# Two transformer blocks in fp32 on one core: another order of work in the last projection, four products with the norm's weights on GpSimd, and weight sums in DRAM that pause

## The reference

```python
branch_d = jnp.einsum('nbsw,nwd->bsnd', ys, w_branch)
g = jax.nn.sigmoid(gates.reshape(bsz, s, N_BRANCH, d))
merged = jnp.sum(g * branch_d, axis=2)
h = x + merged @ w_out            # the last projection
out = rms_norm_2(h, final_g)      # h * rsqrt(mean(h*h) + eps) * final_g
```

## Time and profile before

| | |
|---|---|
| three runs | 1256.29, 1257.59, 1258.3 us; median 1257.59 |
| the profiled execution | 1253.7 us, of which the span of the trace is 1252.0 |
| granted clock, mean | 0.996 |
| busy | PE 1236.2 us, DVE 878.1, ACT 658.7, POOL 84.0 |

### The profile page before, as it was taken

One profiled execution on the slowest core, in us unless ns is written; L12 is line 12 of the kernel. 1 busy time (PEld: TensorE's weight loads), 2 busy tenths in 40 slices (PEclk: granted clock), 3 DMA queues, 4 the chain that ended last, 5 costly groups with the idle time before them and its releaser, 6 DMA issues.

```text
span 1252.0 us, 19450 instructions
## 1 busy us (share of the span) xinstructions
PE 1236.2 (99%) x7427; PEld 1086.2 (87%) x7427; DVE 878.1 (70%) x1560; ACT 658.7 (53%) x1235; POOL 84.0 (7%) x135
## 2 busy tenths in 40 slices
PE   9999999999999999999999999999999999999996
PEld 7887777899999998888888888888898899999985
DVE  5367776697766588788574788765786766665796
ACT  5366676455454455565644224663456774444643
POOL 1000000011010100001200101000000000000000
PEclk9999999999999999999999999999999999999998
DMA  7259888167667755655525888777898886554621
GB/s 253 102 170 252 233 228 223 65 236 232 149 202 226 221 164 179 211 208 185 192 80 162 241 261 239 201 202 235 270 297 270 256 257 223 194 202 169 248 88 68
DMA packets 42141, 253.27 MB, mean 202 GB/s; under 512 B 5304, under 2 KB 6588, under 8 KB 14144
## 3 DMA queue, kind: packets, MB, share of 16 engines
q1 hardware_dynamic: 27096, 161.12, 35.2%
q0 software_dynamic: 11808, 85.99, 28.2%
q10 hardware_dynamic: 3144, 4.92, 1.3%
HBM read 241.51 MB, written 81.80 MB: 258 GB/s over the span
## 4 chain that ended last, share of the span: by engine, by line
PE 92%; DVE 4%; issue 2%; ACT 1%; DMA 1%; POOL 0%; SPq 0%; POOLq 0%; DVEq 0%; ACTq 0%
PE bank L2395 22%; PE bank L2396 22%; PE bank L2397 22%; PE sc L2395 4%; PE sc L2396 4%; PE sc L2397 4%; PE sc L2571 3%; PE tp L2580 2%; PE ob L2637 1%; PE ob L2595 1%; DVE w_lo L1520 1%; PE bank L2512 1%; PE bank L2521 1%; DMA w_raw<-in_weights 1%; PE bank L2502 1%
## 5 line engine op out<-in xcount | busy, mean ns | idle before, releaser
L1520 DVE TENSOR_TENSOR w_lo<-w_raw,w_hi 128x512 fp32r<-128x512 f32 (+1 forms) x417 | 302.2, 772 | 131.6 <-ACT w_hi L910 130.7
L910 ACT ACTIVATE w_hi<-w_raw 128x512 fp32r<-128x512 f32 (+1 forms) x417 | 262.9, 688 | 140.9 <-PE bank L2397 92.3
L2395 PE MATMUL bank<-xT_hi,w_hi 128*128 128x256 f32 (+1 forms) x928 | 319.7, 345 | 0.3
L2397 PE MATMUL bank<-xT_hi,w_lo 128*128 128x256 f32 (+1 forms) x928 | 309.2, 333 | 0.0
L2396 PE MATMUL bank<-xT_lo,w_hi 128*128 128x256 f32 (+1 forms) x928 | 308.9, 333 | 0.0
L2395 PEld LDWEIGHTS bank<-xT_hi,w_hi 128*128 128x128 f32 x928 | 176.3, 190 | 20.3 <-issue 4.6
L2397 PEld LDWEIGHTS bank<-xT_hi,w_lo 128*128 128x128 f32 x928 | 176.1, 190 | 17.7
L2396 PEld LDWEIGHTS bank<-xT_lo,w_hi 128*128 128x128 f32 x928 | 176.5, 190 | 15.3 <-issue 1.0
L2395 PE MATMUL bank<-act_hi,w_hi 128*128 128x256 f32 (+1 forms) x400 | 124.4, 311 | 0.0
L2396 PE MATMUL bank<-act_lo,w_hi 128*128 128x256 f32 (+1 forms) x400 | 123.4, 308 | 0.0
L2397 PE MATMUL bank<-act_hi,w_lo 128*128 128x256 f32 (+1 forms) x400 | 123.3, 308 | 0.0
(11 more groups left out here) (365 smaller groups left out, 2364.5 us busy)
## 6 DMA issues: line engine op xcount, KB each, us to landing
w_raw<-in_weights SPq DMA_DIRECT2D x84, 1024.0 KB, 5.1
sum_dram<-in_weights POOLq DMA_DIRECT2D x54, 1024.0 KB, 8.7
w_raw<-sum_dram SPq DMA_DIRECT2D x34, 1024.0 KB, 4.8
sum_dram<-sum_dram POOLq DMA_DIRECT2D x18, 1024.0 KB, 6.8
arena<-in_weights SPq DMA_DIRECT2D x8, 1024.0 KB, 9.5
act_f<-in_weights POOLq DMA_DIRECT2D x6, 1024.0 KB, 9.9
arena<-in_weights POOLq DMA_DIRECT2D x4, 1024.0 KB, 11.5
act_lo<-act_lo SPq DMA_DIRECT2D x24, 128.0 KB, 5.6
```

What stands on the lines that cost most here:

```text
L910: nc.scalar.activation(w_hi[SPLIT_AT[b]][:, cols], w_raw[SLOT[b]][:, cols], ACT.Copy)\
L1520: nc.vector.tensor_tensor(w_lo[SPLIT_AT[b]][:, cols], w_raw[SLOT[b]][:, cols], w_hi[SPLIT_AT[b]][:, cols].bitcast(F32), ALU.subtract).then ...
L2395: nc.tensor.matmul(ps, hi_l, hi_r, start=first, stop=False, skip_group_check=onto)
L2397: return nc.tensor.matmul(ps, lo_l, hi_r, start=False, stop=last, skip_group_check=onto)
```

## The change

1. DVE's list in the last projection: adds 4 and 5 (product 2) come ahead of make_left("s3") and make_left("s4"), and the split of the last weight block is moved from ahead of them to behind split_left("s4"), in two halves of two parts with an add after the first. The multiplications and variances of the tiles 2 and 3 no longer stand between their adds: all adds up to 14 come first. One entry of OUT_ADDS, product 3's second add from its bank, moves behind the two adds of product 4.
2. ACT's list: round_left("s4") comes ahead of the split of the last block and of the squares; the stores of the tiles 2, 3 stand behind the squares of the tiles 0, 1 (left half) and between the last ones.
3. The four multiplications with the norm's weights for the tiles 2 and 3 go from DVE to POOL, which does the roots in between.
4. POOL waits, ahead of the sums of the group quad3, until PE has done all products of quad0. So the last three groups (quad3, quad4, out: 24 DMAs) begin only then.

```diff
@@ -108,9 +108,10 @@
 AHEAD_AT = (3, 5)
-OUT_ADDS = [(0, 0, 0, 0), (0, 1, 1, 0), (1, 0, 2, 0), (1, 1, 3, 0), (2, 0, 0, 0), (2, 1, 1, 0), (3, 0, 2, 1), (3, 1, 3, 1), (3, 1, 1, 1),
-            (4, 0, 0, 1), (4, 1, 1, 1), (5, 0, 2, 0), (5, 0, 2, 1), (5, 1, 3, 0), (5, 1, 3, 1), (6, 0, 0, 1), (6, 1, 1, 1), (6, 2, 1, 1)]
-OUT_GAINS = [(0, 0), (1, 0), (2, 0), (2, 1), (3, 0), (3, 1), (0, 1), (1, 1), (1, 2)]
+OUT_ADDS = [(0, 0, 0, 0), (0, 1, 1, 0), (1, 0, 2, 0), (1, 1, 3, 0), (2, 0, 0, 0), (2, 1, 1, 0), (3, 0, 2, 1), (3, 1, 3, 1), (4, 0, 0, 1),
+            (4, 1, 1, 1), (3, 1, 1, 1), (5, 0, 2, 0), (5, 0, 2, 1), (5, 1, 3, 0), (5, 1, 3, 1), (6, 0, 0, 1), (6, 1, 1, 1), (6, 2, 1, 1)]
+OUT_GAINS = [(0, 0), (1, 0), (0, 1), (1, 1), (1, 2)]
+OUT_POOL_GAINS = [(2, 0), (2, 1), (3, 0), (3, 1)]
 
@@ -120,6 +121,7 @@
 SUMS_FROM = 8
+SUMS_PAUSE = "quad3"
 LEFT_MADE = [("s1", 0), ("s2", 0), ("s1", 1), ("s2", 1), ("s1", 2), ("s2", 2), ("s4", 0), ("s4", 1), ("s4", 2), ("s3", 0), ("s3", 1), ("s3", 2)]
@@ -520,6 +522,7 @@
         ahead_rounded, ahead_split = sem("ahead_rounded"), sem("ahead_split")
+        pool_gained = sem("pool_gained")
         out_left, out_full, out_added = sem("out_left"), sem("out_full"), sem("out_added")
@@ -778,6 +781,11 @@
 
+            def root(name, t):
+                n = NCOL[name, t]
+                pool.wait_ge(var_done, n + 1)
+                nc.gpsimd.tensor_tensor(rstd[:, n:n + 1], var[:, n:n + 1], minus_half[:, :], ALU.pow).then_inc(rstd_done, 1)
+
             for t in range(2):
@@ -833,6 +841,8 @@
                 for g in groups:
+                    if GROUPS[g] == SUMS_PAUSE:
+                        pool.wait_ge(quad_full, 2 * PRODUCTS)
                     yield from sums_of_weights(g)
@@ -882,7 +892,15 @@
             nc.gpsimd.drain()
-            reciprocal_roots("final")
+            for i, (t, half) in enumerate(OUT_POOL_GAINS):
+                if half == 0 and t != OUT_TILES[0]:
+                    root("final", OUT_TILES[0])
+                cols = slice(W * half, W * half + W)
+                pool.wait_ge(gpost_loaded, 16 * 5)
+                pool.wait_ge(out_added, last_add(t, half))
+                nc.gpsimd.tensor_tensor(out_m[t][:, cols], out_x[:, t, cols], g_post[:, cols], ALU.mult).then_inc(pool_gained, 1)
+            for t in OUT_TILES[1:]:
+                root("final", t)
 
@@ -1477,7 +1495,10 @@
                 act.wait_ge(rstd_done, n + 1)
-                act.wait_ge(out_gained, OUT_GAINS.index((t, 0)) + 1)
+                if t >= 2:
+                    act.wait_ge(pool_gained, OUT_POOL_GAINS.index((t, 0)) + 1)
+                else:
+                    act.wait_ge(out_gained, OUT_GAINS.index((t, 0)) + 1)
                 part = slice(0, out_cut(t))
@@ -1490,19 +1511,20 @@
             round_left("s3")
+            round_left("s4")
             split(FIRST["out"] + 3)
...
                 squares_out("finala", t, last_add(t, 0), left)
-            round_left("s4")
-            for i, t in enumerate(OUT_TILES):
-                if t >= 2:
-                    squares_out("finala", t, last_add(t, 0), left)
-                if t != OUT_TILES[-1]:
-                    squares_out("finalb", t, last_add(t, 1), right)
-                else:
-                    squares_out("finalb", t, last_add(t, 1) - 1, slice(W, W + W // 2))
-                    squares_out("finalc", t, last_add(t, 1), slice(W + W // 2, D))
-                scale_out(i, t)
+            for t in (2, 3):
+                squares_out("finala", t, last_add(t, 0), left)
+                squares_out("finalb", t, last_add(t, 1), right)
+            squares_out("finalb", 0, last_add(0, 1), right)
+            scale_out(0, 2)
+            squares_out("finalb", 1, last_add(1, 1) - 1, slice(W, W + W // 2))
+            scale_out(1, 3)
+            squares_out("finalc", 1, last_add(1, 1), slice(W + W // 2, D))
+            scale_out(2, 0)
+            scale_out(3, 1)
 
@@ -2330,7 +2352,10 @@
                 dve.wait_ge(rstd_done, n + 1)
-                dve.wait_ge(out_gained, max(i for i, (tile, _) in enumerate(OUT_GAINS) if tile == t) + 1)
+                if t >= 2:
+                    dve.wait_ge(pool_gained, OUT_POOL_GAINS.index((t, 1)) + 1)
+                else:
+                    dve.wait_ge(out_gained, max(i for i, (tile, _) in enumerate(OUT_GAINS) if tile == t) + 1)
                 part = slice(out_cut(t), D)
@@ -2347,45 +2372,48 @@
             split_left("s2")
+            add_out(4)
+            add_out(5)
             make_left("s3")
             make_left("s4")
-            split(FIRST["out"] + 3)
-            add_out(4)
-            add_out(5)
             split_left("s3")
-            for n in (6, 7, 8):
-                add_out(n)
+            add_out(6)
+            add_out(7)
+            add_out(8)
             split_left("s4")
+            parts = split_parts(FIRST["out"] + 3)
+            step(parts, 2)
             add_out(9)
+            step(parts, 2)
             add_out(10)
+            add_out(11)
+            add_out(12)
+            add_out(13)
+            add_out(14)
             gain_out(0, 0)
             gain_out(1, 0)
-            begin_variance("final", 0)
-            begin_variance("final", 1)
-            for t in (2, 3):
-                add_out(2 * t + 7)
-                add_out(2 * t + 8)
-                gain_out(t, 0)
-                gain_out(t, 1)
+            for t in range(TT):
                 begin_variance("final", t)
-                variance("final", t, D)
-                scale_out(t)
+                if t >= 2:
+                    variance("final", t, D)
             add_out(15)
...
             variance("final", 0, D)
-            scale_out(0)
 
...
                 gain_out(last, 1 + part)
+                if part == 0:
+                    scale_out(2)
                 k = SCOL["final" + "bc"[part], last]
...
                                                op0=ALU.mult, op1=ALU.add).then_inc(var_done if part else var_begun, 1)
-            scale_out(last)
+            for t in OUT_TILES[1:]:
+                scale_out(t)
 
@@ -2938,7 +2966,7 @@
                 if j >= 4:
-                    pe.wait_ge(out_added, {(4, 0): 5, (4, 1): 6, (5, 0): 10, (5, 1): 11, (6, 0): 7, (6, 1): 2}[j, r])
+                    pe.wait_ge(out_added, {(4, 0): 5, (4, 1): 6, (5, 0): 9, (5, 1): 10, (6, 0): 7, (6, 1): 2}[j, r])
 
```

## The result

The changed kernel takes 1261.31 us (median of 9 runs, 1255.71 to 1266.33), the kernel before 1254.99 us in the runs beside it (9 runs, 1253.36 to 1258.3). The ratio is 1.0049, with a 95% interval of 1.0033 to 1.0065. The prediction was 1253.9 us with a range up to 1260.0 and "faster" as the likeliest: it was wrong. What happened is its rival B. The profiled execution took 1266.33 us, with a span of 1264.5 us, 12.5 longer than before. It is the longest of the nine; the others lost less.

A forecast was written before the change was run, and what follows sets the result against it. PE was taken as the bound, at work for 1236.2 of 1252.0 us. The tail's -3.7 and the pause's 0, from the runs' median, gave 1257.6 - 3.7 = 1253.9 us, range 1250.0 to 1260.0.

The forecast's parts named there:

- rival B: SP's wait at line 739: sums end at 1151.6 or later, 8.50 us each; at 8.6, +5.0, 1262.6 us; chance 0.21.
- I take 8.30: POOL's 24 delayed sum DMAs: 8.30 us each from 947.7, so the last ends at 1146.9.
- the threshold: Before quad4's fourth block load on SP: sums may end as late as 1147.2 without PE waiting.
- the other bound: Sums beside the kernel's loads from 1040 to 1146: 10.2 us each for 13 of them, ending at 1173.
- 0.3 us of room: Sums ending at 1146.9 against the allowed 1147.2, so the pause was taken to cost nothing.
- The price: Late sums: every us beyond 1147.2 is a us of PE; beyond some 2 us the clock's 1.8 is added.
- The tail: Last projection to the span's end: new order and POOL's multiplications end it near 1248.3, 3.7 us earlier.
- the clock's 1.8 us: Last projection's product 4: the lowered clock after PE's wait on an add costs 1.8 us, which the change saves.
- 4.1 of PE: Last projection, adds 4 and 5 earlier: PE saves 2.3 of wait and 1.8 of clock, ending near 1238.5.
- The carried 3.9 us: Median of the runs above the profiled run by 3.9 us, carried over: 1257.6 - 3.7 = 1253.9.
- Rival C: More gain: DVE not held up by POOL (1252.6 us), or quad0 waits in unprofiled runs go too (1250.0); chance 0.13.
- The room of 1.5 us: Quad0, ACT's split at 929.15 waiting 1.54 us for weights: about 1.5 us left until PE would have waited.

The follow-up runs named there:

- the one with the load later: Changed kernel, pause kept, with SP's load of the last sum moved behind three more loads of the last quad: 1250.02 us, ratio 0.9975 to the kernel before.
- the mended one: Kernel before plus the pause, with SP's load of the last sum behind three further loads and the old tail: 1253.11 us, ratio 0.9993.

## Why the prediction was wrong

**The failed step is "I take 8.30" for a sum DMA.** With it the sums end at 1146.9, 0.3 us short of the threshold. They ended at 1160.2. The eleven beside the attention work went at 8.28, as taken (8.4 in the working of the bound); the thirteen beside the loads of quad2 to quad4 took 9.34, between 8.30 and the 10.2 that I had worked out as the other bound. I had judged by the stretch to 946.04, where quad0's loads were in it and the pace was 8.22. That average hid two paces. SP's loads of quad0 begin at 896.84; of before's thirteen steps the seven up to 892.08 took 7.56 us each and the six from there 8.99 (one of them 14.3, the other five 7.94). In the five other profiles whose sums run beside quad0 such steps took 9.1 to 10.0. With 8.99 for the last thirteen and 8.4 for the first eleven the sums would have ended near 1157 (an estimate), well inside rival B. SP's own loads before came to 1 MB every 6.2 us in quad0 (897 to 947), every 8.1 in the attention part (to 1036) and every 5.4 from 1040 to 1146. The cost was one-sided: with 0.3 us of room, and bounds for the end of 19 us earlier and 26 later, 0 was its lower edge and not its middle; rival B, given 0.21, should have had the most.

**The threshold was right to 0.8 us.** Predicted 1147.2. The changed kernel's load at 1160.24 less the 12.0 that PE lost gives 1148.2, and 1146.4 without the 1.8 by which PE was late already; the pause alone gives 1146.5 in the same way (1157.76, 11.4 lost, PE 0.1 early). So the forecast's own 1146.9 lay beyond it, and the 0.3 us of room were none. Loads at 1142.16 and 1144.01 cost nothing. The price was right as well: 13.0 us beyond 1147.2 and 1.8 for the clock make 14.8; 12.0 and 2.3 are 14.3.

**One wait was not in the prediction:** 1.8 us at 1053, where ACT's split at 1051.36 waits 5.97 us for its weights (before, the one at 1048.16 waited for PE alone). It was 0.9 us in the pause alone and 0.5 in the one with the load later, where the sums are beside it too; but also 0.7 in the kernel with POOL's multiplications first, whose last sum is issued at 1036.6; so the sums are not shown to be its only cause.

**The tail was right:** -3.7 predicted, -3.65 measured, and -3.56 to -3.62 in the five other kernels with it. By its steps, with the shift of 16.15 us taken off: PE's last matmul near 1238.5 (measured 1254.51 and 0.1 more, so 1238.5); add 15 at 1236.4 (1236.33); DVE's multiplication longer than 0.7 (1.40), the variance behind it held up too (1.22); last squares at 1242.45 (1241.62, 0.8 earlier); last store 1244.9 (1244.16, 0.7 earlier); end 1248.3 (1248.35, since 4.2 us lie behind the last store and not 3.4). Two small errors cancel. That POOL and DVE exclude one another was right, as the multiplications that POOL holds up in one order are short in the other; even a 128x1 instruction takes 1.22 us instead of 0.16. This is the rule of the Trainium skill ("SBUF — State Buffer", section "SBUF: two separate sides"), and the trace agrees with it. That the clock's 1.8 us belong to every execution of before was too much: behind the same wait it was 0.63 in before and 0.67 in the pause alone, and 1.00 in the mended one (and 0.63 behind the wait of the two adds alone, one product later). The move of the two adds by itself shortened the tail by 0.2 us, where the prediction credits it with 4.1 of PE: the new place of the split in DVE's list belongs to that step.

**The carried 3.9 us were wrong.** The medians of before were 1254.99, 1253.71, 1254.17 and 1255.00 in groups of 9 to 35 runs; the three runs at hand were high ones, and the profiled 1253.7 was near the middle. The tail alone would have been 1253.7 to 1255.0 less 3.7, 1250.0 to 1251.3; it was 1250.0 to 1250.8.

**Rival C in part:** in three profiles with sums beside quad0 or just ahead of it PE waited 0.6 to 1.8 us there (1.4, 1.8, 0.6), in the others, that of before among them, not. With the clock such a wait can cost more than twice its length, as the 3.6 us for 1.4 above. The room of 1.5 us that I counted there is used up in some executions. The mended pause shows that this is worth too little to be measured.

## What to carry to other kernels

Before a transfer is moved later, look for who waits for it and what stands behind that waiter in its queue; if what stands behind does not need it, reorder the queue first; here the delay was then free. A margin that is smaller than the spread of the pace it rests on is no margin: take such a cost from its middle, not from the edge at zero. In a list of adds and splits that feeds another engine, moving one item forward can move the wait to the next item; count what that engine needs one product further on.

## What the runs showed of the hardware

- The 24 sum DMAs of 1.05 MB, one at a time, take 192.5 to 204.6 us from first to last issue in seven profiles that differ little beside them. Beside the attention part they took 7.5 to 8.5 us each, averaged over ten or eleven steps; beside the denser loads of SP 8.8 to 9.6 in the last quads (ten to twelve steps, seven profiles) and 9.0 to 10.0 in quad0 (five or six steps, six profiles). A total of 284 GB/s at a DMA share of 0.90 is not the most: one profile with a shorter pause moved 295 at 0.92 in the same window.
- They slow the other side down as well: from 1040 to 1140 SP's weight loads landed 7.0 to 7.7 us after their issue (medians of the two kinds), before 4.8 and 4.9; in quad0, from which the sums were taken, 4.8 instead of 6.8 to 7.0.
- While POOL multiplies 128x512 from SBUF (2.55 us for two, 2.96 for two beside DVE), DVE's instructions with both inputs in SBUF stand still, a 128x1 one for 1.1 us. Its adds with one input in PSUM pass: two of them take 1.28 us from 1249.27 on, as elsewhere, with POOL at work from 1247.39 to 1249.94.
- The granted clock falls in the course of a long wait: it was 0.81 from 1158 to 1162, in a wait that began at 1157.15, and is 0.51, near the lower level, for the 5.3 us behind it. Short waits can do it too: 0.66 for 5.0 us behind one of 1.43, and behind one of 2.16 in two profiles and not in a third, with the same matmuls ahead of the wait.
